# Block 1's attentions, gating, gates and output: from eight stages to one

## The reference, cut to what matters

```python
h = rms_norm(x, g_mix[i])
(a_q, a_k, a_v, s_z, s_x, s_b, s_c, s_dtf, s_dtb, c_q, c_k, c_v, d_uv) = split(h @ w_in[i])
q, k = axial_rope(rms_norm(a_q), ...), axial_rope(rms_norm(a_k), ...)   # 4 and 2 heads of 64
o_a = gqa_block_attention(q, k, a_v)                # softmax attention over all 512 keys
o_b = bidir_ssd(s_z, s_x, s_b, s_c, ...)            # convolution, decays, two-way scan, norm
o_c = diff_block_attention(...)                     # 4 heads: softmax1 - lam * softmax2, with a bias
o_c = rms_norm(o_c, g_diff[i]) * (1 - lam_init)
o_d = spatial_gating(d_uv, ...)                     # gelu, norm of a half, 4 products 128x128, product
gates = sigmoid(h @ w_branch_gate[i])               # 4 branches of 1024
merged = sum over n of gates[n] * (o_n @ w_branch[i, n])     # o_n is 512x256
x = x + merged @ w_out[i]
```

## Time and profile before

| | |
|---|---|
| median of 3 runs (4468.8 to 4471.5) | 4471.2 us |
| profiled execution, its span | 4469.6 us, 4467.8 us |
| busy in the span: PE, DVE, ACT | 83%, 39%, 24% |
| mean granted TensorE clock | 0.904 |

### The profile page before, as it was taken

How to read it: one execution, slowest core, us unless ns; L and a number is a source line. 1 busy time by engine, 2 the same in 40 slices (tenths; PEclk the granted TensorE clock), 3 DMA queues, 4 the chain that set the end, 5 groups by cost and what they waited for, 6 DMA issues and landing times. The chain is left out here.

```text
span 4467.8 us, 45450 instructions
## 1 busy us (share of the span) xinstructions
PE 3723.3 (83%) x17444; PEld 2471.1 (55%) x17444; DVE 1733.7 (39%) x3050; ACT 1063.9 (24%) x1631; POOL 24.3 (1%) x34
## 2 busy tenths in 40 slices
PE   5757799699976946799699997598989968998998
PEld 4634577334435824577444344376666656666666
DVE  2377333311123267533311113234764332367443
ACT  2133222000012233322100002333333213333321
POOL 0010000000000001000000000000000000000000
PEclk9875899899998966699899998798999989999999
DMA  3100221899962200122599991411112241111222
GB/s 128 48 2 1 86 92 53 329 414 412 409 282 83 70 5 2 61 89 81 203 408 409 412 409 56 181 57 38 58 66 71 95 179 57 39 48 57 81 71 94
DMA packets 133313, 640.70 MB, mean 143 GB/s; under 512 B 23457, under 2 KB 46497, under 8 KB 66833
## 3 DMA queue, kind: packets, MB, share of 16 engines
q1 hardware_dynamic: 127888, 629.83, 36.5%
q10 hardware_dynamic: 5248, 8.52, 0.6%
HBM read 629.78 MB, written 8.53 MB: 143 GB/s over the span
## 5 line engine op out<-in xcount | busy, mean ns | idle before, releaser
L2098 PE MATMUL ps<-normed_T_hi,ring_split 128*128 128x512 f32 (+1 forms) x1952 | 639.6, 409 | 40.7 <-PEq L283 14.5
L2098 PEld LDWEIGHTS ps<-normed_T_hi,ring_split 128*128 128x128 f32 (+1 forms) x1952 | 370.6, 193 | 154.5 <-issue 44.7
L2098 PE MATMUL ps<-normed_T_lo,ring_split 128*128 128x512 f32 (+1 forms) x976 | 388.8, 398 | 0.0
L1419 PE MATMUL ps<-normed_T_hi,ring_split 128*128 128x512 f32 x1024 | 343.5, 417 | 0.0
L1695 PE MATMUL ps<-weight_ring,projected 128*64 128x512 f32 x1280 | 281.0, 593 | 15.4 <-DVE projected L1740 15.4
L2374 DVE TENSOR_TENSOR ring_split<-weight_ring,ring_split 128x2048 fp32r<-128x2048 f32 x76 | 174.0, 2290 | 301.9 <-ACT ring_split L2259 301.8
L272 PE MATMUL ps<-weights_hi,normed_T_hi 128*128 128x472 f32 (+1 forms) x512 | 199.6, 390 | 46.3 <-DVE weights_lo L362 46.3
L1419 PEld LDWEIGHTS ps<-normed_T_hi,ring_split 128*128 128x128 f32 x1024 | 193.6, 189 | 69.6 <-issue 29.7
L2098 PEld LDWEIGHTS ps<-normed_T_lo,ring_split 128*128 128x128 f32 (+1 forms) x976 | 187.6, 192 | 42.7
L1419 PE MATMUL ps<-normed_T_lo,ring_split 128*128 128x512 f32 x512 | 201.5, 394 | 0.0
L1758 DVE TENSOR_TENSOR residual<-residual,ps 128x512 f32<-128x512 f32 x128 | 88.1, 688 | 290.5 <-PE ps L1716 290.5
(11 more groups left out here) (397 smaller groups left out, 6014.2 us busy)
## 6 DMA issues: line engine op xcount, KB each, us to landing
weight_ring<-in_w_exp_gate SPq DMA_DIRECT2D x96, 1024.0 KB, 20.5
weight_ring<-in_w_slabs SPq DMA_DIRECT2D x78, 1024.0 KB, 4.9
spare_weights<-in_w_exp_up SPq DMA_DIRECT2D x64, 1024.0 KB, 26.0
weight_ring<-in_w_exp_up SPq DMA_DIRECT2D x64, 1024.0 KB, 11.8
spare_weights<-in_w_exp_down SPq DMA_DIRECT2D x64, 1024.0 KB, 17.9
weight_ring<-in_w_branch_gate SPq DMA_DIRECT2D x32, 1024.0 KB, 4.9
weight_ring<-in_w_exp_down SPq DMA_DIRECT2D x32, 1024.0 KB, 14.5
weight_ring<-in_w_ada SPq DMA_DIRECT2D x16, 1536.0 KB, 12.5
```

Of the source, the lines that this page charges most:

```text
L1419: ins = e.matmul(dst, lhs(k, m), rhs(k, m), start=k == 0 and m == 0, stop=stop and k == KD - 1 and m == 2)
L2098: ins = e.matmul(dst, lhs(k, m), rhs(k, m), start=k == 0 and m == 0, stop=k == KD - 1 and m == 2)
```

## The change

The scan chain (`conv_stage`, `decay_stage`, `scan_stage`) moves to just behind the projection. Queries' norm, both attentions, lambda, the second attention's norm, spatial gating, the turns and the mix become one stage, `late_stage`. One list `order` holds the dense steps (turns, spatial products, gates, output steps) and the chain parts ("qk_sum", "attend", "gelu_a", ...), and every engine walks through it.

- Dense steps use PSUM banks 0 and 1 in turn: a step waits until the one two before it is evicted. The branch products use bank 7, the logits 2 and 3, the turned weights 4 and 5, the weighted values 6. The first three dense steps are two turns of the scan's result and the turn of the spatial weights.
- 24 attention jobs: 8 of the first (two heads of a token tile at once), 16 of the second. `attend(j)` on TensorE turns the weights of job j-2, weighs job j-3 and does the logits of job j. On VectorE it finishes job j-4, scales the weights of j-2 and takes the maxima of j-1; on ScalarE it does the exponentials of j-1 and copies the turned weights of j-2.
- The branches are gated in the order 1, 3, 0, 2 (scan, spatial, first attention, second).
- The sigmoid becomes 0.5 (1 + tanh(x/2)); VectorE adds the 1, and the 0.5 goes into the last scaling of the merged sum. 0.125, the first attention's scale, goes into the queries' norm.
- The merged sum is accumulated in `X`'s room; the residual is stored to HBM by the norm that opens the layer, and read back after the last merged part, before the first output step is evicted.
- The branch weights use the room of `rope_T`; block 2's table is now loaded by the norm between the blocks and not at the start.
- All small loads (16) are issued by SP behind the first three slabs.

```diff
-            norm_stage([(gain_col, columns("g_mix", l))], gain_col)
+            norm_stage([(gain_col, columns("g_mix", l))], gain_col, save=True)
             project_stage(a["w_in"][l, :, :], 0, 6, 472, IN1)
-            qk_stage(l)
...
-            attention_stage([pair_a(r) for r in range(2)], [(0, 64)], all_keys, 0.125)
             conv_stage(l)
             decay_stage(l)
             scan_stage(l)
-            lambda_stage(l)
-            attention_stage([pair_c(p) for p in range(2)], [(0, 32), (32, 64)], all_keys, 32 ** -0.5,
-                            bias=lambda h, t: bias_tiles[:, h, 384 - P * t:896 - P * t], lam=small[:, 134:135])
-            diff_norm_stage(l)
-            spatial_stage(l)
-            branch_at = (Z_XBC, Z_XBC + P, 0, P, D_UV, D_UV + P)
-            turn_stage(lambda t, k: Z[:, t, branch_at[k]:branch_at[k] + P], BRT[:, 2:8, :], 6)
-            mix_stage(4, 2, BRT, ...)
+            late_stage(l)
```

The order in `late_stage` (chain parts between the dense steps):

```diff
+            turn(("brt", 2), Z_XBC, BRT[:, 2, :], "V")
+            turn(("brt", 3), Z_XBC + P, BRT[:, 3, :], "S")
+            step("turn", "S", ("wst",), srcs=[ws[:, g, :] for g in range(4)], dst=wst[:, :, :], after=("inputs_loaded", 256))
+            for t in range(NT):
+                place("qk_sum", t)
+            place("qk_var")
+            place("gelu_a", 0)
+            place("gelu_a", 1)
+            gate(0)
+            place("qk_rstd")
...
+            gate(1)
+            place("gelu_b")
+            place("qk_scale", 0)
+            gate(2)
...
+            gate(4)
+            place("gelu_var")
+            place("qk_scale", 3)
+            place("gelu_rstd")
+            turn(("q", 0), A_QK, QK[:, 0, :], "S", after=("stage_a", NT))
+            turn(("k", 0), A_QK + 256, QK[:, 2, :], "V")
+            turn(("q", 1), A_QK + P, QK[:, 1, :], "S")
+            gate(5)
+            place("lam_a")
+            place("attend", 0)
+            for g in range(4):
+                step("spatial", "V", ("spatial", g), g=g)
+            place("lam_b")
+            gate(6)
+            place("attend", 1)
...
+            for j in range(3, 28):
...
+                if j in (4, 6, 8) or 10 <= j <= 26 and j not in (13, 16, 19, 22, 25, 26):
+                    gate(steps[-1]["g"] + 1 if steps[-1]["kind"] == "gate" else max(st["g"] for st in steps if st["kind"] == "gate") + 1)
+                place("attend", j)
+            place("diff_a")
+            gate(22)
+            place("diff_b")
+            gate(23)
+            turn(("brt", 4), 0, BRT[:, 4, :], "S", after=("stage_b", NT))
+            turn(("brt", 5), P, BRT[:, 5, :], "V")
+            for g in range(24, 32):
+                gate(g)
+            for i in range(16):
+                step("out", "V", None, i=i, t=i % 4, slab=16 + i // 4)
```

SP's queue and the waits of TensorE's dense steps and attends:

```diff
+                    for q in range(3):
+                        e.dma_start(ring_land[:, q, :], a["w_branch_gate"][l, 4 * branch_of[q // 4] + q % 4, :, :]).then_inc(landed[q], 16)
+                    e.dma_start(ws, a["w_spatial"][l, :, :, :].rearrange("g t n -> t g n")).then_inc(s["inputs_loaded"], 16)
+                    for h in range(6):
+                        e.dma_start(qk_gain[:, h, :], a["g_qnorm" if h < 4 else "g_knorm"][l, :].partition_broadcast(P)).then_inc(s["inputs_loaded"], 16)
...
+                    load_side(0)
+                    load_side(1)
+                    for q in range(3, slabs):
+                        if q == 19:
+                            e.wait_ge(s["merged_ready"], KD)
+                            e.dma_start(X[:, :, :], x_saved.rearrange("(t p) d -> p t d", p=P)).then_inc(s["x_loaded"], 16)
+                        e.wait_ge(s["dense_ready"], last_of[q - 3] + 1)
...
+                    def dense(i):
+                        st = steps[i]
+                        kind, b = st["kind"], i % 2
+                        if i >= 2:
+                            e.wait_ge(s[steps[i - 2]["taken"][0]], steps[i - 2]["taken"][1])
+                        if "slab" in st:
+                            e.wait_ge(s["slab_lo"], st["slab"] + 1)
...
+                        if kind == "gate":
+                            g, n, q = st["g"], st["n"], st["slab"]
+                            e.wait_ge(side_landed[q % 2], 16 * (q // 2 + 1))
+                            if g:
+                                e.wait_ge(s["gate_used"], g)
...
+                        if 2 <= j < J + 2:
+                            turn_probs(j - 2)
+                        if 3 <= j < J + 3:
+                            weigh(j - 3)
+                        if j < J:
+                            logits(j)
```

```diff
+                            if g < KD:
+                                e.scalar_tensor_tensor(sums[:, c, :], v, 1.0, PS[:, 7, :], ALU.add, ALU.mult).then_inc(s["gate_used"], 1)
...
+                            e.scalar_tensor_tensor(v, v, 1.0, PS[:, 7, :], ALU.add, ALU.mult).then_inc(s["gate_used"], 1)
...
+                            e.tensor_tensor(sums[:, c, :], sums[:, c, :], v, ALU.add).then_inc(s["gate_done"], 1)
```

The table of block 2, in `row_norm_stage`:

```diff
+                    if not store:
+                        e.dma_start(rope_T[:, :, :], a["c_rope_T"]).then_inc(s["side_landed"], 16)
+                        e.wait_ge(s["side_landed"], 16)
```

More of the change, by code:

```diff
@@ L481, in rope_tile @@
             e.tensor_tensor(x, ta, tmp_b.rearrange("p (h d) -> p h d", h=heads), ALU.add).then_inc(s[step], st.add(step))
[L484 to L529, removed]
@@ L1103, in _ @@
                     e.wait_ge(s[st.name], st.value)
-        def lambda_stage(l):
-            s = signals.stage()
-            v = T[:, 0:128].rearrange("p (i n) -> p i n", i=4)
-            pr = T[:, 128:192].rearrange("p (i n) -> p i n", i=2)
-            init, dots, ex, lam = small[:, 128:130], small[:, 130:132], small[:, 132:134], small[:, 134:135]
-            with nc.Block() as block:
-                @block.sync
-                def _(e):
-                    signals.zero_other(e)
-                    for i, name in enumerate(("lambda_q1", "lambda_q2", "lambda_k1", "lambda_k2")):
-                        e.dma_start(v[:, i, :], a[name][l, :].partition_broadcast(P)).then_inc(s["inputs_loaded"], 16)
-                    e.dma_start(init, a["c_lam"][l, :].partition_broadcast(P)).then_inc(s["inputs_loaded"], 16)
-                    e.wait_ge(s["inputs_loaded"], 80)
-                @block.scalar
-                def _(e):
-                    e.wait_ge(s["stage_a"], 1)
-                    e.activation(ex, dots, ACT.Exp).then_inc(s["stage_b"], 1)
-                @block.vector
-                def _(e):
-                    st = Tally()
-                    e.wait_ge(s["inputs_loaded"], 80)
-                    e.tensor_tensor(pr, v[:, 0:2, :], v[:, 2:4, :], ALU.mult).then_inc(s["vector_step"], st.add("vector_step"))
-                    e.wait_ge(s[st.name], st.value)
-                    e.tensor_reduce(dots, pr, AX_X, ALU.add).then_inc(s["stage_a"], 1)
-                    e.wait_ge(s["stage_b"], 1)
-                    e.tensor_tensor(lam, ex[:, 0:1], ex[:, 1:2], ALU.subtract).then_inc(s["vector_step"], st.add("vector_step"))
-                    e.wait_ge(s[st.name], st.value)
-                    e.tensor_tensor(lam, lam, init[:, 0:1], ALU.add).then_inc(s["vector_step"], st.add("vector_step"))
-                    e.wait_ge(s[st.name], st.value)
@@ L2625, in mixer_kernel @@
         with nc.Fori(0, DEPTH) as l:
-            norm_stage([(gain_col, columns("g_mix", l))], gain_col)
+            norm_stage([(gain_col, columns("g_mix", l))], gain_col, save=True)
             project_stage(a["w_in"][l, :, :], 0, 6, 472, IN1)
-            qk_stage(l)
-            Z = z_view(IN1)
-            BRT = R[:, 0:4096].rearrange("p (k n) -> p k n", k=8)
-            def pair_a(r):
-                q = lambda t: Z[:, t, A_QK + P * r:A_QK + P * (r + 1)]
-                return dict(q=q, k=lambda t: Z[:, t, A_QK + 256:A_QK + 384], v=lambda hh, kb: Z[:, kb, A_V + 64 * hh:A_V + 64 * hh + 64], heads=(r, 2 + r), out=BRT[:, r, :])
-            def pair_c(p):
-                return dict(q=lambda t: Z[:, t, C_Q + P * p:C_Q + P * (p + 1)], k=lambda t: Z[:, t, C_K + P * p:C_K + P * (p + 1)],
-                            v=lambda hh, kb: Z[:, kb, C_V + P * p + 64 * hh:C_V + P * p + 64 * hh + 64], heads=(2 * p, 2 * p + 1),
-                            out=lambda hh, t: Z[:, t, P * p + 64 * hh:P * p + 64 * hh + 64])
-            attention_stage([pair_a(r) for r in range(2)], [(0, 64)], all_keys, 0.125)
             conv_stage(l)
```

969 lines of the change are left out of this document (469 added, 500 removed).

## The result

The changed kernel takes 4321.86 us (median of 4 runs, 4318.64 to 4325.04) against 4470.01 (4463.06 to 4471.5, 4 runs) of the kernel before on the same chip: a ratio of 0.9672, interval 0.9655 to 0.9688. The profiled executions have spans of 4323.3 and 4467.8 us, 144.5 apart; the two new stages account for 69.3 + 74.6 = 143.9 of that, so the rest of the kernel moved by 0.6 us in sum. Single stretches of it moved by up to 1.6 us, either way: layer two's scan chain is 1.6 longer here, and 1.4 longer in the experiment that moves that chain alone.

What follows compares the result with a forecast made beforehand. Mix bound by TensorE at full clock, earlier stages by chains of waiting engines. Terms 25 + 276.5 + 74 + 24 + 6 + 10 + 0.5 = 416 us against 481.7 and 482.7, 132.4 less in both layers: 4336 us, range 4275 to 4395.

Steps and rivals of the forecast that it cites:

- The start: New stage's start: TensorE waits for sixteen small loads, 25 us a layer; 20 if flights overlap, 31.5 behind three slabs.
- Dense work: New stage: 32 gates of 7.2 us, 230.3, and output matmuls, 46.2, make 276.5 us a layer; counts unchanged.
- Attention, turns and spatial products on TensorE: New stage: first attention 26.5, second 40, turns and spatial products 7.8; 74 us a layer.
- Stalls: New stage: TensorE's waits beside VectorE and ScalarE work, 24 us a layer, bounds 10 to 45.
- the thirteen microseconds in the plain attends: Attends with no gate between: 1.6 us in five places of the second attention, 1.2 in four of the first.
- the sign of 8 to 18 us: From first gate matmul to last gate: TensorE's waits for the scaled weights would sum to 8 to 18 us.
- The residual's reload: Output steps: the first eviction waits for the residual read back from HBM, 6 us a layer; 2 to 6.6.
- The clock: New stage: 10 us a layer at the lower clock, 4 at gate 0 and 6 behind stalls; bounds 3 to 25.
- The convolution: Outside the stage: following the projection at full clock, its first turns gain about 1 us a layer.
- (a): Rival: nearly all is hidden; start 20, stalls 12, clock 4, so 393 us a layer, 4288 us; chance 0.14.
- (b): Rival: VectorE's chain paces the second attention, 40 us more a layer, 4416 us; chance 0.10 with other stalls.
- (c): Rival: slower, clock stays at the lower level through the attends; 169 us a layer more, 4675 us; chance 0.06.

Runs made afterwards that it cites:

- the ballast: The changed kernel with one more reduction of 512 columns on VectorE in each of the 16 jobs of the second attention: 4319.39 us, ratio 0.9668.

## Why the prediction was right

Layer one, term by term, predicted against measured:

- *The start*, 25 (bounds 20 to 31.5): 27.9, and 22.8 in layer two, 25.4 in the mean. That the mean comes so near is in part luck, since the prediction took the layers to be alike. The wait is for the small loads, as said. The rate of the earlier trace rows, 1.47 us a load, is what the experiment with two gain loads for six measured (1.5 to 1.6). The upper end, 31.5, came in neither layer. The slabs' packets (8 KB each, 384 in all) do go first, as the packets of layer one show, from 286.2 to 296 and from there to 313.5:

```profile
DMA packets 527, 3.20 MB, mean 326 GB/s; under 512 B 44, under 2 KB 143, under 8 KB 143
DMA packets 4015, 1.41 MB, mean 81 GB/s; under 512 B 2978, under 2 KB 4015, under 8 KB 4015
```

  But behind the slabs the small loads needed some 17.5 us, and 12.5 in layer two, not the 23.5 that the upper end adds to the 8; nine of the sixteen had been issued while the slabs still moved. The Trainium skill (DMA: Bandwidth & Descriptors, section Queues, rings and completion order) says that each DMA engine takes its descriptors in ring order. The trace agrees with that order; what was too long is the sum that the prediction made of it.
- *Dense work*, 276.5: the counts are those of before. Gates woven between attends run at 7.3 and 7.7 us without their waits in the stretch shown (these two, three attends of 2.48 and the 1.6 of waits make the 24.0), against 7.2 predicted.
- *Attention, turns and spatial products on TensorE*, 74: 74.2. Added from the start of each such group to the start of the dense step behind it they take 83.7 us, 9.5 of it waits. An attend of the second attention takes 2.48 (2.5 predicted), one of the first 3.1 (3.3).
- *Stalls*, 24 (10 to 45): the step that was mis-sized most. The waits of the list above, without the two ahead of gate 0 and the reload, and with those of 0.3 to 0.6 that follow in it, sum to 15.7. It was the thirteen microseconds in the plain attends: measured were 6.2 in nine places, 0.7 each, where I had taken 1.6 and 1.2, the former from block 2's mean in the earlier trace rows. They also miss the sign of 8 to 18 us that the prediction named for them. VectorE was further ahead than I allowed: with the ballast 8 us more work on it were absorbed.
- *The residual's reload*, 6 (2 to 6.6): 4.9 and 5.3, in the third output step as said. Its landing was used 8.5 us after the issue (646.06 to 654.59), 9.4 in the earlier trace rows.
- *The clock*, 10 (3 to 25): 412.4 less all of the above leaves 13.2 for the clock, the tail and the slightly longer gates, 10.5 predicted for the first two. The lower level stood where a start or a stall went ahead; the windows of the changed kernel are the start, gate 0's first matmuls, the gates with attends, and the stretch behind the last attends (the one behind the reload stands above):

```profile
286.30:306.30 20.00, 1.91 (x8) 1.51 (x8) 12.45 (x18) 4.42 (x4) 0.00 (x0) 0.50 0.57 199
306.30:316.30 10.00, 2.84 (x9) 2.48 (x10) 3.83 (x8) 1.70 (x2) 0.00 (x0) 0.50 0.24 64
...
320.30:560.00 239.70, 227.44 (x1100) 156.39 (x1099) 146.82 (x269) 91.14 (x178) 0.00 (x0) 1.00 0.17 57
563.00:573.00 10.00, 9.59 (x37) 8.07 (x37) 4.72 (x6) 5.67 (x6) 0.00 (x0) 0.66 0.00 1
```

  Of the 10, 4 were for gate 0, up to 5.5, a bound for which the prediction gives no row. By the trace it was some 2 (an estimate: its first nine gate matmuls took 4.0 us, 314.20 to 318.19, where nine later took 2.0). Some 3.4 went behind the last attends (10 us at 0.66) and 2.5 behind the reload.

The errors: 2.9 + 0.2 - 8.3 - 1.1 + 2.7 = -3.6, that is 416 to 412.4; in layer two the start gives 5.1 back, and longer waits elsewhere take a part of it, so that its 408.1 lies 7.9 below. So a part of the agreement is that errors of either sign met.

Outside: the store in the norm costs nothing (15.0 us for 15.2), as said. The convolution did not gain its 1 us a layer (31.4 us in both): that step failed. Its group of turns on TensorE after the change, busy time, mean ns, idle time before it:

```profile
L218 PE MATMUL ps<-constants,weight_ring 128*128 128x128 f32 x16 | 3.7, 424 | 23.8 <-DVE weight_ring L551 23.8
```

Busy time, mean duration and idle time are those of before: these turns do not run at a higher clock than there, and TensorE's long wait there is for VectorE.

The rivals. (a), 393 a layer, was too low for the start and the clock, but its stalls (12) were nearer than mine. (b) falls: VectorE's chain does not set the pace, by the experiment with the ballast. (c) falls: the clock is 0.94. Its mechanism is real, though: with twelve gates taken from between the attends, TensorE ran at 0.50 for 79 us. The order in which the two are mixed prevents that, which is worth 27 us a layer.

Not settled is why the small loads take 5.1 us longer in layer one than in layer two. SP issues the last of them at the same point in both; it lands 8.3 us after its issue in layer one and 3.5 in layer two. With the branch weights first and the gates ahead the difference disappears from the time.

## What to carry to other kernels

Count what a merged stage's first step waits for, in the order of the issuing queue: here sixteen small loads held TensorE for 20 to 25 us of each stage, and moving one step and two loads gave back 16 of them. Weave small matmuls with large ones even if hardly a wait is saved: what they lost here by standing alone was the clock, 27 us a layer. When a stall is priced, add the lower clock behind it (here 2.5 us on 4.9), and when a mean wait is borrowed from another stage, ask first how far ahead the waited-for engine is in this one.

## What the runs showed of the hardware

- A wait of TensorE of 4.9 us cost 7.4: behind it the matmuls ran at the lower level for 4.6 us (655.1 to 659.7).
- Small loads that broadcast one row to 128 partitions cost 1.5 to 1.6 us each when several stand in a row on SP's queue, and their issue holds SP (4.62 us for two at 298.03).
- A table load of ScalarE took 1.28 us; 36 of them in a stage, in place of three, cost the kernel 19.5 us a stage. In layer one's profile 9.3 of it was idle time of TensorE and 11.5 longer matmuls.
